# Attention of the first layer: TensorE issues the scores of two units together

## The reference

```python
s_band = jnp.einsum('bnqcgd,bnscd->bncgqs', qb, kb).astype(jnp.float32) * scale + b_band
s_band = jnp.where(valid[None, :, None, None, None, :], s_band, -jnp.inf)
s_meta = jnp.einsum('bnqcgd,bmcd->bncgqm', qb, km).astype(jnp.float32) * scale + b_meta
p = sink_softmax(jnp.concatenate([s_meta, s_band], axis=-1), sinks...)
o = (jnp.einsum('bncgqm,bmcd->bnqcgd', p[..., :META], vm)
     + jnp.einsum('bncgqs,bnscd->bnqcgd', p[..., META:], vb))
```

## Time and profile before

| | us |
|---|---|
| median of three runs | 2892.44 |
| the three runs | 2887.47, 2892.44, 3653.46 |
| the profiled execution | 2886.49 |
| its span, first to last instruction | 2884.7 |
| attention of layer 1 | about 171 to 359 |
| VectorE, ScalarE, POOL busy in the whole span | 1522.2, 700.9, 906.2 |

### The profile page before, as it was taken

The page is one execution under the profiler, slowest core; times in us unless marked ns, Lnnn a source line. Parts: engine busy times, 40 slices in busy tenths (PEclk is TensorE's granted clock), DMA queues, the critical chain, the costliest instruction groups (busy, mean ns, idle before and its releaser), DMA issues. The chain is left out here.

```text
span 2884.7 us, 47310 instructions
## 1 busy us (share of the span) xinstructions
PE 2814.6 (98%) x18301; PEld 2658.3 (92%) x18301; DVE 1522.2 (53%) x2779; ACT 700.9 (24%) x1500; POOL 906.2 (31%) x860
## 2 busy tenths in 40 slices
PE   8999999999999999999889999999999999999997
PEld 7988799999999999998579877789999999999997
DVE  6146616444544444456588878533644554444455
ACT  4037611000000000003467666631100000000002
POOL 2233333222222222224024754323222222222232
PEclk9999999999999999999999999999999999999999
DMA  4530011111111111114012000021111111111112
GB/s 126 75 92 12 20 37 37 45 37 44 33 40 44 44 44 38 42 42 129 8 32 62 28 11 10 21 79 41 44 37 44 44 36 44 44 36 44 44 37 76
DMA packets 178207, 129.80 MB, mean 45 GB/s; under 512 B 25313, under 2 KB 168353, under 8 KB 177846
## 3 DMA queue, kind: packets, MB, share of 16 engines
q1 hardware_dynamic: 178066, 127.90, 15.6%
HBM read 111.13 MB, written 15.16 MB: 44 GB/s over the span
## 5 line engine op out<-in xcount | busy, mean ns | idle before, releaser
L1259 POOL CAST w_hi<-w_raw 128x1024 fp32r<-128x1024 f32 x120 | 145.0, 1209 | 1098.9 <-PE ps_gemm L1503 600.3
L704 DVE TENSOR_TENSOR h<-h,ps_gemm 128x1170 f32<-128x1170 f32 (+1 forms) x192 | 262.5, 1367 | 371.2 <-PE ps_gemm L1519 208.5
L1503 PE MATMUL ps_gemm<-xh,w_hi 128*128 128x390 f32 (+1 forms) x1920 | 445.8, 340 | 0.0
L1503 PE MATMUL ps_gemm<-xl,w_hi 128*128 128x390 f32 (+1 forms) x1920 | 444.9, 340 | 0.0
L1503 PE MATMUL ps_gemm<-xh,w_lo 128*128 128x390 f32 (+1 forms) x1920 | 444.7, 340 | 0.0
L1503 PEld LDWEIGHTS ps_gemm<-xh,w_hi 128*128 128x128 f32 x1920 | 349.2, 189 | 0.1
L1503 PEld LDWEIGHTS ps_gemm<-xl,w_hi 128*128 128x128 f32 x1920 | 348.1, 189 | 0.0
L1503 PEld LDWEIGHTS ps_gemm<-xh,w_lo 128*128 128x128 f32 x1920 | 348.0, 189 | 0.0
L1262 POOL TENSOR_TENSOR w_lo<-w_raw,w_hi 128x1024 fp32r<-128x1024 f32 x120 | 290.5, 2421 | 17.4
L712 ACT ACTIVATE ac<-ac 128x1184 f32<-128x1184 f32 x44 | 52.5, 1194 | 857.8 <-DVE ac L771 857.8
L1464 PE MATMUL ps_gemm<-xl,w_hi 128*128 128x390 f32 (+1 forms) x1056 | 246.5, 342 | 0.0
(11 more groups left out here) (424 smaller groups left out, 4649.6 us busy)
## 6 DMA issues: line engine op xcount, KB each, us to landing
w_raw<-in_w_gate SPq DMA_DIRECT2D x44, 512.0 KB, 3.8
w_raw<-in_w_up SPq DMA_DIRECT2D x44, 512.0 KB, 3.8
w_raw<-in_w_down SPq DMA_DIRECT2D x44, 512.0 KB, 3.4
w_raw<-in_w_in_b SPq DMA_DIRECT2D x13, 512.0 KB, 4.0
w_raw<-in_w_qkv_a SPq DMA_DIRECT2D x10, 512.0 KB, 4.2
residual_park<-h SPq DMA_DIRECT2D x1, 4680.0 KB, 13.6
h<-residual_park SPq DMA_DIRECT2D x8, 585.0 KB, 7.3
out<-yt SPq DMA_DIRECT2D x9, 512.0 KB
```

The costliest lines, as they stand in the source:

```text
L704: dve.tensor_tensor(c3(h[:, m, :], l), c3(h[:, m, :], l), pse(j, l), ALU.add).then_inc(evac[j % 2], 1)
L1259: pool.tensor_copy(whi[c % 3][:], raw[c % 2][:]).then_inc(w_hi_done, 1)
L1503: mm = pe.matmul(ps[j % 2][:, m_, 0:ch], w[:, k, :], x[:, k, x0 + m_ * ch:x0 + (m_ + 1) * ch], start=(k == 0 and w is wh and x is XH), sto ...
```

## The change

In layer 1 (`layer` 0), scores are issued only in even turns: in turn n those of units n and n+1, one behind the other, before the groups of turn n. In an odd turn TensorE begins with keys or transposes. Layer 2 keeps its order. No other engine's program changes, and no semaphore count does. `lead()` still stands before the scores of turn 2.

```diff
                 for n in range(NU + LAG):
                     if n == 2:
                         lead()
-                    if n < NU:
-                        scores(n)
+                    for i in range(n, n + 1) if layer else range(n, n + 2) if n % 2 == 0 else ():
+                        if i < NU:
+                            scores(i)
                     gs = AT[layer][n]
                     if gs and gs[0]["keys"] is not None:
                         keys(gs[0])
```

## The result

| | before | after |
|---|---|---|
| median of 13 runs, us | 2891.49 | 2901.72 |
| ratio, 95% interval | | 1.0037 [1.0029, 1.0044] |
| profiled execution, us (span) | 2886.49 (2884.7) | 2898.23 (2896.5) |

The changed kernel is slower by 0.37%, about 10 us: under the 2% that a verdict asks for, but clear of the noise of 13 runs. The ratio leaves out the one run of before with 3653.46 us, and the 13 runs of after lie in two groups, six from 2895.85 to 2898.40 us with the profiled one among them and seven from 2901.72 to 2905.19. I had forecast 2898 us: 9.4 us for the change above the profile of before, and 2.1 us for the distance from that profile to the median.

A forecast was written before the change was run, and what follows sets the result against it. TensorE was taken to bound the first layer's attention. 7.9 us for 30 pairs plus 1.5 for early ones made +9.4 on the profiled 2886.49, 2895.9; 2.1 more for the median gave 2898 us, range 2882 to 2919.

The forecast's parts named there:

- What bounds the stage: First layer's attention, 171 to 359 us: TensorE runs without a stop and the other engines stand ready behind it.
- 0.11 us saved a pair: TensorE's scores directly behind scores take 0.44 instead of 0.55 us; 36 pairs gain 4.0 us if nothing waits.
- The least stall, 0.21 us: Scores(n+1) wait for VectorE's late reduce(n-1,1), released 0.86 us after the pair's start; +0.10 us a pair after the saving.
- The loop of 5.11 us: Scores through finish, reduction, exponential, reciprocal, copy, finish and reduction to scores(n+3): 5.11 us a pair against 4.74, +0.37.
- Transposes behind the waiting scores: Part of the 5.11 us loop: transposes counted 0.76 us after the start of scores(n+1).
- The 14 turns: Turns 18 to 31, a repeating pattern of seven pairs with stream units: +1.85 us in sum.
- The last pair: Turns 30/31: finish is behind the reduction, so no stall and -0.11 us.
- The first tile: Five or six pairs before turn 12, smaller blocks, loop without the second copy: +0.3 us each, 1.5 us.
- stands on no path: POOL's work on the outputs follows finish, with the next finish over 2 us later, so it was to delay nothing.
- No stall (1): Rival: scores go through without waiting and only the saved changes count, -4 us, 2882.5 us; chance 0.18.
- A larger stall (2): Rival: ScalarE's copy or exponential delays exp(n,1), up to 23 us over 36 pairs, 2910 to 2919 us; chance 0.19.
- The clock (3): Rival: TensorE's waits lower its granted clock, under 1.00 between 190 and 354 us; chance 0.02.

The follow-up runs named there:

- e1: Changed kernel, with VectorE in the first layer doing reduce(n,1) directly behind reduce(n,0); ratio to before 0.9992, 14 turns 34.58 us.
- e4: Changed kernel, with VectorE doing reduce(n,1) before the second third of its groups in even first-layer turns only; ratio to before 1.0027, 14 turns 36.03 us.
- e8: e1 with the five bias-band fills on VectorE spread over turns 4 to 7; ratio to before 0.9978, stage 182.70 us.

## Why the prediction was right, and where it was only nearly so

- **What bounds the stage.** Held: TensorE did, and what it now waits is what the kernel lost. One of the reasons was misread. The chain that ended last covers 33% of the span and begins at 1889 us, far behind this stage, so it says nothing of it. The waits carry the argument alone.
- **0.11 us saved a pair.** Held in ordinary pairs: 1.41 instead of 1.52 us from the first scores to the transposes in e1. A period of seven pairs saves 0.67 us, against 7 x 0.11 = 0.77. Two of the seven pairs hold a stream unit and save almost nothing: in e1 an ordinary unit and a stream behind it take 0.76 + 0.43 us, where each alone takes 0.76 and 0.44. That leaves 0.55. Keys that directly follow products give back about 0.10 (they start 0.70 us after the products, 287.81 to 288.51 in e1, where I had 0.80).
- **The least stall, 0.21 us.** Held: 0.20 to 0.22 us in four of seven pairs of e4. That the mean of all seven, +0.11, also meets the +0.10 of an ordinary pair is luck; the other three are 0.09, 0.47 and 0.02 over e1.
- **The loop of 5.11 us.** Held: 5.17 in the pair shown, link by link. The price of 0.53 us for the release of the scores was borrowed from ScalarE; TensorE's was 0.56.
- **Transposes behind the waiting scores.** The loop of 5.11 us has the transposes start behind scores(n+1), ready or not; the rows of before, where no score waits, could not show this. In the pair shown it held: the last exponential that these transposes read was through at 270.64 us and the last copy out of their banks at 271.34, but TensorE stood for 0.51 us, started the scores at 272.00 and the transposes at 272.76.
- **The 14 turns.** Predicted +1.85 us, measured +2.00. The sum is closer than its pairs, and that is luck. What after takes more than e1 is the stall; the prediction's figure with the 0.11 put back is its forecast. From units 19 to 21 on: 0.31 for 0.37, 0.69 for 0.48, 0.44 for 0.48, 0.47 for 0.54, 0.21 for 0.27, 0.35 for 0.48, 0.21 for 0. The last pair was to have no stall, since its finish is behind the reduction; it has one.
- **The first tile.** This is the term that was mis-sized: I estimated 1.5 us for the five pairs, +0.3 each, and all up to unit 17 cost 4.9 us, where my figures give about 2.3 (1.5 and three pairs of 0.26). With the fills spread, so without the long wait and the lower clock behind it, it is still 4.6 us, and the stalls of these pairs are 0.66 to 1.26 us where I had 0.41 (0.3 and the 0.11 saved). I had shortened the steady loop by a copy. The rows show another loop, through POOL, of which I had written that it "stands on no path": 5.36 us from the scores at 196.41 to those at 201.77. The forecast had not seen the fills either, with their wait of 2.55 us; but they cost the kernel before nearly as much (1.8 us) as the changed one (2.1).
- **The rivals.** No stall (1): refuted. A larger stall (2): not in the steady part, where the stalls of seven pairs are 2.7 us against e1 and 2.6 by my figures, and TensorE's waits for ScalarE's keys grew only from 1.5 to 2.2 us. In the early pairs the stalls are larger; the one read above passes through POOL. The clock (3): for the steady part refuted, 1.00 as forecast, from 212 to 364 us of after with waits of up to 0.51 us. But behind the one wait of 2.55 us the clock did fall, between 192 and 196 us. At 0.57 over 4 us that costs at most 1.7 us (an estimate from this row), and not the 58 us that a verdict asks for.
- **The total.** 9.4 us forecast over the profile; the profiles differ by 11.7 us and the medians by 10.2. That 2898 is near 2901.72 is partly luck. The early turns cost 2.6 us more than thought. The allowance of 2.1 us from profile to median was too small: it was 5.0 us for before and 3.5 for after.

## What to carry to other kernels

Moving an instruction forward on the engine that bounds a stage is safe only as far as its wait was slack: take the place where its releaser ends now, follow the releaser's own queue backwards, and look whether that queue holds something which waits for the moved engine's last work. If it does, you have closed a loop, and its length is a sum of rows you can read beforehand. Do it for each part of the stage whose turns are laid out differently; the loop of the early turns went through a fourth engine. The same loop tells the cheap cure: e1 moved one reduction forward on the other engine and took the 10 us of loss away (ratio 0.9992, with 1 in its interval). With the fills spread too it is a gain (0.9978 and 0.9976).

## What the runs showed of the hardware that I had not expected

TensorE's clock fell behind a single gap, in after and in e1. With 2.55 us of waiting (1.45 us busy in 4) the granted clock was 0.57 in the following 4 us in after; with a wait of 2.02 us in e1 it was 0.77 from 188 to 192 us, which hold the wait, and then 0.50; in e8, with the fills spread, it stayed 1.00 there. From 212 to 364 us of after, with waits of up to 0.51 us, it was 1.00. The waits alone do not tell when it falls: behind waits of 1.60 and 0.58 us it was 0.58 in e4, behind 1.60 and 0.57 us it was 1.00 in after. The stretch with the stall cost more than the wait was long: from unit 5 to 9, e1 with its wait of 2.02 us took 12.66 us and e8 7.91.
